# Mixing the first output tile inside the unit stage, opening the conv units' slots without a barrier, and a new order of the output stage

## The chip, the cores and the metric

The kernel runs on one core of one Trainium2 chip. The metric is the device time of one execution in microseconds (us). It computes in fp32 with matmuls on pairs of fp16 parts.

## What is computed

Two layers of a decoder, for one prompt of 2048 tokens and eight samples of eight tokens each. A layer is, cut to what matters here:

```python
h = rmsnorm(x, g_pre)
(...) = split_cols(h @ w_in)          # columns of four head groups
# A: short gated conv, B: gated linear attention, C: window attention, D: memory attention
mix = jnp.concatenate([a_out, b_out, c_out, d_out], axis=-1) @ w_out
y = x + rmsnorm(mix, g_post)
```

`y` of layer 0 is `x` of layer 1. The width is 1024.

## The kernel before

The tokens go through in four passes, of 1024 prompt tokens each: layer 0 first half, layer 0 second half, layer 1 first half, layer 1 second half. The second-half passes (2 and 4) also carry the 64 sample tokens. A pass has two stages, `units` (L1456) and `out` (L3018). Each of the five engines (TensorE or PE, ScalarE or ACT, VectorE or DVE, GpSimd or POOL, and SyncE or SP, which only issues transfers) goes through its own list in order and waits on semaphores.

**The unit stage.** `plan_units` (L461) writes one list of items with a forecast of each engine's time (`Forecast`, L171), and every engine walks the same list. Projections (`proj`, L2021) are cut in pieces between the attention work. The work of the head groups is divided into 16 slots; `begin` and `end` items open and close them. A `begin` that isn't `joined` makes PE, ACT, DVE and POOL wait until all four have ended the slot before (`all_steps_done`, L1642). Slots 8 and 9 and the last two, 14 and 15, belong to the conv units A; nearly all of the work of these is done by then, so that they hold no work in passes 1 and 3, and in passes 2 and 4 slot 15 holds two small transposes. At the end the planner places `o_split` (the last parts of `w_out`, split into a high and a low fp16 part by ACT and DVE, L2427 and L2676), `o_load` (in passes 2 and 4: kept parts of `w_out`, L1961, issued once slot 13 has ended on all engines), `o_x` (the next pass's first two rows of `x` and the norm weights `pre_g`, L1970 and L1971) and `o_mix`: the mix of the first output tile is split into `m_hi` (ACT, L2431) and `m_lo` (DVE, L2680). `o_mix` comes after slot 14. PE posts `left` after its last slot, once the PSUM banks 2 to 7 have been read (L2042).

**The output stage.** Its order is one hand-written list, `order` (L3056), of which each engine takes its share in that order. An output tile `t` is 128 tokens; there are 8, and 9 in passes 2 and 4, where tile 6 is the 64 sample tokens. The entries are:

- `("o", t, n)`: half `n` of the tile's product with `w_out` (PE L3147, 24 matmuls of 512 columns; sample tile L3136, 16), and ACT's sum of squares (L3214). For the sample tile ACT first copies the lower rows (L3208) and DVE adds them (L3274).
- `("mix", t)`: the split of mix tile `t` (ACT L3192, DVE L3259).
- `("fin", t)`: DVE's closing of a tile (L3280 to L3293, POOL's root L3119 between them), after which the tile's two banks are free for tile `t + 2` (L3295).
- `("xn", u)`: the next pass's norm of row tile `u`: ACT squares (L3180), DVE L3243 and L3244, POOL L3119, DVE L3248.
- `("h", u)`: the turn of that row tile (PE L3163, 8 transposes), ACT `h_hi` (L3223), DVE `h_lo` (L3303), and ACT's load of row tile `u + 2`.
- `("split", i)`: in passes 1 and 3, a part of `w_out` that the unit stage left over (one part, number 6; ACT L3196, DVE L3263). PE's second halves `("o", t, 1)` need the high and the low part of it (L3145).

There are no `xn` and `h` entries in pass 4, and in pass 2 there are eight of each (0 to 7). Passes 1 and 3 turn nine row tiles, of which the last is the samples. SP waits for all `left`, clears the unit stage's semaphores, and loads `post_g` and the first residual rows (L3077, L3079).

Of the kernel before, what the change touches and what calls it, by code (L numbers as in the profile page):

```python
# [33 lines left out]
ALU = mybir.AluOpType  # L34
# [426 lines left out]
def plan_units(with_sample):  # L461
# [137 lines left out]
    n_kept = [0]  # L599
    last_on_pe = [None]  # L600
# [215 lines left out]
    def follow():  # L816

        emit_parts()
        while raws and raws[0][0] <= fc.t["PE"]:
            wscale()  # L820
        while landing and max(landing[0][0], fc.at.get(("scaled", landing[0][1]), landing[0][0] if landing[0][1] < RING else float("inf"))) <= fc.t["PE"]:
            wsplit()
        while lows and lows[0][0] <= max(fc.t["PE"], fc.t["POOL"]):
            wlow()
        while out_landing and out_landing[0][0] <= fc.t["PE"] and (out_landing[0][1] >= RING or begun >= len(slots) - (2 if with_sample else 4)):
            emit(item("o_split", part=out_landing.pop(0)[1]))
        while waiting and rows_ready(waiting[0]) and rows_rest(waiting[0]):
            evict_next()
        while ahead and (max(ahead[0][0], fc.needs(ahead[0][1])) <= fc.t["PE"] + EARLY or not (left[ahead[0][1]["group"]] or running)):
            it = ahead.pop(0)[1]  # L830
            emit(it)
            turning[it["group"]] -= 1
# [35 lines left out]
    while ended < len(slots):  # L868
        follow()
        now = fc.t["PE"]  # L870
        if ended <= begun and not left[slots[ended]["index"]] and not any(x["step"]["slot"] == ended for x in main + side if "step" in x):
            emit(item("end", slot=ended, steps=[slots[ended]["main"]] + slots[ended]["side"]))
            ended += 1
            running = ended <= begun
            if not with_sample and ended == len(slots) - 4:
                out_loads += [2, 3]
                out_load("o_load", 0, after=ended)
                out_load("o_load", 1, after=ended)
            if with_sample and ended == len(slots) - 4:
                for part in (2, 3):  # L880
                    emit(item("o_load", part=part, after=ended))
            if with_sample and ended == len(slots) - 2:
                for part in (0, 1):
                    emit(item("o_load", part=part, after=ended))
            if ended == len(slots) - 2:
                emit(item("o_x"))
            if ended == len(slots) - 1:
                emit(item("o_mix"))
            continue
        if not running and not main:  # L890
            x = slots[begun + 1]
            if not (unread[x["index"]] or turning[x["index"]] or (heads and heads[0]["step"]["slot"] == x["index"])):
                main.append(item("begin", slot=x["index"], steps=[x["main"]] + x["side"], joined=False))
# [87 lines left out]
def hymba_step(nc, x_prompt, x_sample, state_conv, state_gla, cache_swa_k, cache_swa_v, cache_mem_k, cache_mem_v,  # L981
# [474 lines left out]
    def units(no, l, second, build, stored_so_far):  # L1456
# [527 lines left out]
        def on_tensor(pe):  # L1984
# [4 lines left out]
            for it in items:  # L1989
# [51 lines left out]
                elif kind == "end":  # L2041
                    if it["slot"] == n_slots - 1:  # L2042

                        for b in range(2, 8):
                            pe.wait_ge(bank_free[b], plan["uses"][b])
                        pe.drain().then_inc(left["pe"], 1)
                    else:
                        pe.drain().then_inc(step_pe, 1)
# [314 lines left out]
        def on_scalar(act):  # L2363
# [5 lines left out]
            for it in items:  # L2369
# [45 lines left out]
                elif kind == "end":  # L2415
                    if any(x["unit"] == "B" for x in it["steps"][1:]):

                        act.wait_ge(stored, 16 * stores)
                    act.drain().then_inc(left["act"] if it["slot"] == n_slots - 1 else step_act, 1)
# [8 lines left out]
                elif kind == "o_mix":  # L2428

                    all_steps_done(act, n_slots - 1)  # L2430
# [587 lines left out]
    def out(no, l, second, build, plan, n_stores):  # L3018
# [37 lines left out]
        order = [("xn", 0), ("mix", 1), ("o", 0, 0), ("h", 0), ("xn", 1)] + [("split", i) for i in late]  # L3056
        order += [("o", 1, 0), ("h", 1), ("xn", 2), ("o", 0, 1), ("fin", 0), ("mix", 2), ("o", 1, 1), ("h", 2), ("xn", 3), ("fin", 1), ("mix", 3)]
        for t in range(2, tiles - 2):
            order += [("o", t, 0), ("xn", t + 2), ("o", t, 1), ("h", t + 1), ("fin", t), ("mix", t + 2)]
        u, v = tiles - 2, tiles - 1  # L3060
        order += [("o", u, 1), ("h", u + 1), ("xn", u + 2), ("o", v, 1), ("h", u + 2), ("next",), ("o", u, 0), ("fin", u)]
# [61 lines left out]
        def on_tensor(pe):  # L3123
            for x in order:
                if x[0] == "o":
                    _, t, n = x
                    b = out_bank(t, n)
                    if t >= 2:
                        pe.wait_ge(out_free[b], t // 2)
# [19 lines left out]
                    m.then_inc(out_full[b], 1)  # L3149
                elif x[0] == "h":  # L3150
# [19 lines left out]
        def on_scalar(act):  # L3170
# [3 lines left out]
            for x in order:  # L3174
# [7 lines left out]
                elif x[0] == "mix":  # L3182
# [3 lines left out]
                    if t == 1:  # L3186

                        for e in ("pe", "dve"):
                            act.wait_ge(left[e], no)
                    if t >= 2:  # L3190
                        act.wait_ge(out_full[out_bank(t, 1)], t // 2)
# [38 lines left out]
        def on_vector(dve):  # L3230
# [3 lines left out]
            if build is not None:  # L3234
                dve.wait_ge(pre_in, 16)
                link(ts(pre_g, pre_g, H_UP, None, ALU.mult))
            for x in order:
                if x[0] == "xn":
                    u = x[1]
                    r = size(u)  # L3240
                    z = st_h[0:r, u % 2]
# [7 lines left out]
                elif x[0] == "mix":  # L3249
# [5 lines left out]
                    if t >= 2:  # L3255

                        dve.wait_ge(out_full[out_bank(t, 1)], t // 2)
# [176 lines left out]
```

## Time and profile before

| what | value |
|---|---|
| three runs | 2083.31, 2091.59, 2093.31 us; median 2091.59 us |
| the profiled execution's own time | 2083.04 us |
| its span, first to last instruction | 2081.2 us |
| mean granted TensorE clock | 0.981 |

The span leaves 1.8 us around it. The profiled execution lies 8.6 us under the median of the three. In the rows below, times are us from the span's start; a row of the timeline has the start, the duration, the engine, the line, the operation, the operands and the count of what is merged in it, and in brackets the engine's idle time before it and what ended it. A merged row's duration ends with the modelled end of its last matmul, so the next row may begin somewhat earlier.

### The profile page before, as it was taken

The page shows a single profiled execution, that of the slowest core. Times are in us where ns is not written, and L with a number is a line of the kernel's source. Part 1 is how long each engine was busy: PE and PEld are TensorE (multiplying, and loading weights), DVE is VectorE, ACT ScalarE, POOL GpSimd, SP SyncE. Part 2 cuts the span into 40 slices and gives each one's busy share as a digit, 9 for nine tenths or more (in the row PEclk, how much of TensorE's full clock was granted, in tenths as well). Part 3 has the DMA queues.
Part 4 walks back from the last instruction along what each step waited for, and adds up shares of the span by engine and source line. Part 5 has one row for each costly group of instructions (what it writes and reads, how often), then busy time and mean ns, then how long its engine had stood idle before and what let it go on. Part 6 is the DMA issues. An engine that isn't in the chain of part 4 may idle for free. (4 is left out here: it accounts for less than half of the span.)

```text
span 2081.2 us, 42790 instructions
## 1 busy us (share of the span) xinstructions
PE 1964.5 (94%) x16314; PEld 1114.3 (54%) x16314; DVE 1278.5 (61%) x2845; ACT 881.4 (42%) x2175; POOL 331.4 (16%) x251
## 2 busy tenths in 40 slices
PE   9999899989999999998999997998999999999998
PEld 5455444445566666665544554444445676566643
DVE  5577675666357775555646776566644677747533
ACT  4555343544355333344436443354435453424322
POOL 1443324000000000000114343320100000000000
PEclk9999999999999999999999999999999999999999
DMA  7731245555621133365356232546554112434632
GB/s 264 185 102 44 81 102 142 132 169 190 165 62 33 47 85 97 86 144 162 137 146 157 72 87 67 138 106 156 197 185 107 62 33 64 98 83 108 144 113 91
DMA packets 327494, 241.66 MB, mean 116 GB/s; under 512 B 188630, under 2 KB 273116, under 8 KB 327260
## 3 DMA queue, kind: packets, MB, share of 16 engines
q1 hardware_dynamic: 324180, 228.34, 40.4%
q10 hardware_dynamic: 3112, 10.59, 1.6%
q8 instruction: 131, 2.15, 0.4%
q14 instruction: 71, 0.58, 0.1%
HBM read 136.60 MB, written 57.71 MB: 93 GB/s over the span
## 5 line engine op out<-in xcount | busy, mean ns | idle before, releaser
L2021 PE MATMUL bank<-h_hi,w_parts 128*128 128x512 f16 (+4 forms) x4240 | 835.1, 344 | 30.9 <-ACTq L2409 15.5
L2021 PEld LDWEIGHTS bank<-h_hi,w_parts 128*128 128x128 f16 (+1 forms) x4240 | 400.5, 98 | 383.3 <-issue 75.5
L2021 PE MATMUL bank<-h_lo,w_parts 128*128 128x512 f16 (+3 forms) x2160 | 436.1, 344 | 0.9
L2021 PEld LDWEIGHTS bank<-h_lo,w_parts 128*128 128x128 f16 (+1 forms) x2160 | 207.0, 98 | 176.4 <-issue 9.7
L3147 PE MATMUL bank<-scr_h,tb_h 128*128 128x512 f16 x768 | 177.6, 391 | 14.5 <-ACT tb_h L2431 9.5
L3147 PE MATMUL bank<-w_parts,tb_h 128*128 128x512 f16 x768 | 170.4, 380 | 1.6 <-DVEq L3295 1.6
L2408 ACT ACTIVATE tb<-bank 128x512 f32<-128x512 f32 (+1 forms) x140 | 71.9, 514 | 190.3 <-PE bank L2021 186.7
L2977 POOL TENSOR_SCALAR w_raw<-w_raw 128x1024 f32<-128x1024 f32 x46 | 131.9, 2875 | 74.9 <-DMA w_raw<-in_w_in 74.3
L3147 PEld LDWEIGHTS bank<-scr_h,tb_h 128*128 128x128 f16 x768 | 76.4, 100 | 107.3 <-issue 12.4
L2972 POOL TENSOR_TENSOR w_parts<-w_raw,w_parts 128x1024 f16<-128x1024 f32 x46 | 100.9, 2196 | 205.2 <-ACT w_parts L2381 204.4
L3214 ACT ACTIVATE junk<-bank 128x512 bf16<-128x512 f32 (+1 forms) x68 | 40.6, 597 | 219.3 <-PE bank L3147 206.7
L2543 ACT ACTIVATE bank<-bank,stat 128x256 f32<-128x256 f32 x256 | 113.7, 447 | 44.0 <-DVE stat L2906 43.6
L3147 PEld LDWEIGHTS bank<-w_parts,tb_h 128*128 128x128 f16 x768 | 74.9, 98 | 91.0 <-DVEq L3295 2.6
L2757 DVE COPY_PREDICATED scr<-level_mask,bank 128x128 f32<-128x128 uint8 (+1 forms) x332 | 116.6, 351 | 11.3
L2404 ACT ACTIVATE tb<-bank 128x512 f32<-128x512 f32 (+1 forms) x80 | 40.9, 511 | 154.5 <-PE bank L2021 121.8
L2994 POOL TENSOR_TENSOR stat_g<-stat_g,minus_half 128x8 f32<-128x8 f32 (+1 forms) x20 | 29.2, 1462 | 457.0 <-DVE stat_g L2805 457.0
L2655 DVE SCALAR_TENSOR_TENSOR tb<-tb,gate_raw 128x512 f32<-128x512 f32 (+1 forms) x80 | 54.4, 680 | 48.6 <-ACT gate_raw L2405 45.5
L2931 DVE SCALAR_TENSOR_TENSOR scr_h<-bank,stat,scr_h 128x256 f16<-128x256 f32 x160 | 66.2, 475 | 15.7 <-ACT scr_h L2554 14.4
L2554 ACT ACTIVATE scr_h<-bank,stat 128x256 f16<-128x256 f32 x160 | 62.8, 490 | 12.1 <-DVE stat L2918 11.1
L2753 DVE COPY_PREDICATED scr<-diag_mask,bank 128x256 f32<-128x256 uint8 (+1 forms) x68 | 29.6, 436 | 53.4 <-ACTq L2489 43.4
L2946 DVE SCALAR_TENSOR_TENSOR mix_t<-bank,tb 128x256 f32<-128x256 f32 x64 | 27.0, 423 | 55.1 <-PE bank L2321 31.7
L2494 ACT ACTIVATE scr<-bank 128x128 f32<-128x128 f32 (+1 forms) x68 | 18.5, 272 | 98.5 <-PE bank L2162 86.9
(338 smaller groups left out, 2723.6 us busy)
## 6 DMA issues: line engine op xcount, KB each, us to landing
w_in_kept<-w_parts SPq DMA_DIRECT2D x104, 256.0 KB, 3.2
w_parts<-w_in_kept SPq DMA_DIRECT2D x104, 256.0 KB, 2.9
w_raw<-in_w_in SPq DMA_DIRECT2D x48, 512.0 KB, 4.2
out<-scr SPq DMA_DIRECT2D x32, 512.0 KB, 2.6
scr<-in_x_prompt SPq DMA_DIRECT2D x16, 512.0 KB, 4.1
scr<-out SPq DMA_DIRECT2D x16, 512.0 KB, 4.4
rot<-out ACTq DMA_DIRECT2D x12, 512.0 KB, 4.0
mix_t<-in_x_prompt SPq DMA_DIRECT2D x8, 512.0 KB, 11.9
```

What stands on the lines that cost most here:

```text
L2021: m = mm(bank[b][0:m_w, 0:c1 - c0], w[:, k, 0:m_w], h[:, k, c0:c1], start=it["piece"] == 0 and k == 0, stop=it["piece"] == 2 and k == KT - 1)
L2404: fn(part_of(s, "z", pt), src, ACT.Tanh, scale=0.5 * UNSCALE).then_inc(tanh_done, 1)
L2408: fn(part_of(s, role, pt), src, ACT.Copy, scale=scale).then_inc(tile_copied, 1)
L2543: m = fn(at, at, ACT.Exp, bias=z[:, 4 + x:5 + x], scale=1.0 if unit == "C" else HD ** -0.5, accum_out=z[:, 12 + x:13 + x])
L2554: m = fn(hi[:, 256 * x:256 * x + 256], scores_of(it["of"], x), ACT.Copy, scale=z[:, 20 + x:21 + x])
L2655: link(stt(z, z, 1.0, raw_gate(span, pt), ALU.add, ALU.mult))
L2757: m = nc.vector.copy_predicated(a.rearrange("p h (m i r) -> p h m i r", i=2, r=v)[:, :, :, 1, :], mask.to_broadcast([w, 2, w // (2 * v), v ...
L2931: m = stt(lo[:, part], scores_of(it["of"], x), z[:, 20 + x:21 + x], hi[:, part], ALU.mult, ALU.subtract)
L2972: tt(lo_of(t), w_raw[:, t % RING, :, 0:split_width(t)], hi_of(t), ALU.subtract).then_inc(w_lo_done, 1)
L2977: nc.gpsimd.tensor_scalar(raw, raw, W_UP, None, ALU.mult).then_inc(w_scaled, 1)
L3147: m = nc.tensor.matmul(bank[b].rearrange("p (j n) -> p j n", j=RING), lhs[:, t % 2, k, :], rhs[:, :, k, :], start=j == 0 and k == 0, stop= ...
L3214: link(fn(junk[0:r], bank[out_bank(t, n)][0:r], ACT.Square, accum_out=st_o[0:r, t % 2, n:n + 1]))
```

## The change

`o_mix` is placed as soon as slot 12 has ended and the gate of conv unit A1's first half is in the list, and ACT then waits only for the slots up to 12 and for that gate. The `begin` of a slot that holds only units A is joined, and so waits for nobody. PE no longer waits for the banks at the end of its last slot: it takes banks 2 and 3 ahead of the first half tile of the output stage, banks 4 to 7 after it, and posts `left` there; ACT posts its own `left` after PE's last slot. The order of the output stage is rewritten: the first turn comes after three half tiles, `xn` stands one tile ahead of its turn instead of two (the one ahead of the last loop's end comes after the loop), and `mix` comes ahead of `fin`. The planner's list of pass 1 and 3 is otherwise made by the same rules, with the changed forecast.

```diff
@@ plan_units
+    mixed = [False]
@@ follow()
+        if not mixed[0] and ended >= len(slots) - 3 and ("evict", slots[-2]["main"]["n"], "z") in placed:
+            emit(item("o_mix"))
+            mixed[0] = True
@@ the planner's loop
             if ended == len(slots) - 2:
                 emit(item("o_x"))
-            if ended == len(slots) - 1:
-                emit(item("o_mix"))
             continue
...
             if not (unread[x["index"]] or turning[x["index"]] or (heads and heads[0]["step"]["slot"] == x["index"])):
-                main.append(item("begin", slot=x["index"], steps=[x["main"]] + x["side"], joined=False))
+                free = x["main"]["unit"] == "A" and all(s["unit"] == "A" for s in x["side"])
+                main.append(item("begin", slot=x["index"], steps=[x["main"]] + x["side"], joined=free))
@@ units, on_tensor, kind "end"
-                    if it["slot"] == n_slots - 1:
-
-                        for b in range(2, 8):
-                            pe.wait_ge(bank_free[b], plan["uses"][b])
-                        pe.drain().then_inc(left["pe"], 1)
-                    else:
-                        pe.drain().then_inc(step_pe, 1)
+                    pe.drain().then_inc(step_pe, 1)
@@ units, on_scalar, kinds "end" and "o_mix"
+                    if it["slot"] == n_slots - 1:
+
+                        act.wait_ge(step_pe, n_slots)
                     act.drain().then_inc(left["act"] if it["slot"] == n_slots - 1 else step_act, 1)
...
-                    all_steps_done(act, n_slots - 1)
+                    all_steps_done(act, n_slots - 3)
+                    gate_written(act, next(x["n"] for x in plan["steps"] if (x["unit"], x["g"], x["st"]) == ("A", 1, 0)))
                     fn(m_hi[:, 0], mix_t[:, :, 0:P], ACT.Copy, scale=M_UP).then_inc(mh_done, 1)
@@ out
-        order = [("xn", 0), ("mix", 1), ("o", 0, 0), ("h", 0), ("xn", 1)] + [("split", i) for i in late]
-        order += [("o", 1, 0), ("h", 1), ("xn", 2), ("o", 0, 1), ("fin", 0), ("mix", 2), ("o", 1, 1), ("h", 2), ("xn", 3), ("fin", 1), ("mix", 3)]
-        for t in range(2, tiles - 2):
-            order += [("o", t, 0), ("xn", t + 2), ("o", t, 1), ("h", t + 1), ("fin", t), ("mix", t + 2)]
+        first_o = ("o", 0, 0)
+        order = [("mix", 1), ("xn", 0), ("o", 0, 0), ("xn", 1)] + [("split", i) for i in late]
+        order += [("o", 1, 0), ("o", 0, 1), ("h", 0), ("mix", 2), ("fin", 0), ("o", 1, 1), ("h", 1), ("xn", 2), ("mix", 3), ("fin", 1)]
+        order += [("o", 2, 0), ("h", 2), ("xn", 3), ("o", 2, 1), ("h", 3), ("mix", 4), ("fin", 2)]
+        for t in range(3, tiles - 2):
+            order += [("o", t, 0), ("xn", t + 1), ("o", t, 1), ("h", t + 1), ("mix", t + 2), ("fin", t)]
         u, v = tiles - 2, tiles - 1
-        order += [("o", u, 1), ("h", u + 1), ("xn", u + 2), ("o", v, 1), ("h", u + 2), ("next",), ("o", u, 0), ("fin", u)]
+        order += [("xn", u + 1), ("o", u, 1), ("h", u + 1), ("xn", u + 2), ("o", v, 1), ("h", u + 2), ("next",), ("o", u, 0), ("fin", u)]
@@ out, on_tensor
+                    if x == first_o:
+                        for b in range(2, 4):
+                            pe.wait_ge(bank_free[b], plan["uses"][b])
...
+                    if x == first_o:
+
+                        for b in range(4, 8):
+                            pe.wait_ge(bank_free[b], plan["uses"][b])
+                        pe.drain().then_inc(left["pe"], 1)
@@ out, on_scalar, "mix" (on_vector likewise waits for both halves at t >= 2)
-                        for e in ("pe", "dve"):
-                            act.wait_ge(left[e], no)
+                        act.wait_ge(left["dve"], no)
                     if t >= 2:
-                        act.wait_ge(out_full[out_bank(t, 1)], t // 2)
+                        for n in range(2):
+                            act.wait_ge(out_full[out_bank(t, n)], t // 2)
@@ out, on_vector
-            if build is not None:
-                dve.wait_ge(pre_in, 16)
-                link(ts(pre_g, pre_g, H_UP, None, ALU.mult))
...
+                    if u == 0:
+                        dve.wait_ge(pre_in, 16)
+                        link(ts(pre_g, pre_g, H_UP, None, ALU.mult))
```

## Rows read from the trace of the kernel before

**Rows 1.** The page: busy time of the engines

```profile
PE 1964.5 (94%) x16314; PEld 1114.3 (54%) x16314; DVE 1278.5 (61%) x2845; ACT 881.4 (42%) x2175; POOL 331.4 (16%) x251
```

**Rows 2.** PE's waits, whole span: us in total, times, longest us

```profile
PE bank L3147 <- ACT tb_h L2431: 9.5, 2, 4.8
...
PE bank L3147 <- DMA scr_h<-w_out_kept: 5.0, 2, 2.6
...
PE bank L2021 <- PEq L2048: 3.8, 4, 1.3
...
PE bank L3163 <- DVE rot L3248: 3.7, 3, 1.8
```

**Rows 3.** Timeline of PE in pass 1's output stage

```profile
435.61 7.04 PE L3147 MATMUL bank<-scr_h,tb_h 128*128 128x512 f16 x24 [4.76 <-ACT tb_h L2431]
444.01 1.09 PE L3163 MATMUL bank<-ident,rot 128*128 128x128 f32 x8 [1.35 <-DVE rot L3248]
...
473.45 5.34 PE L3147 MATMUL bank<-scr_h,tb_h 128*128 128x512 f16 x24
...
483.81 1.04 PE L3163 MATMUL bank<-ident,rot 128*128 128x128 f32 x8
```

**Rows 4.** Timeline of PE in pass 2's output stage

```profile
966.16 8.09 PE L3147 MATMUL bank<-scr_h,tb_h 128*128 128x512 f16 x24 [2.42 <-DMA scr_h<-w_out_kept]
...
1037.03 1.04 PE L3163 MATMUL bank<-ident,rot 128*128 128x128 f32 x8
1037.91 3.62 PE L3136 MATMUL bank<-scr_h,tb_h 128*128 128x512 f16 x16
...
1044.81 1.04 PE L3163 MATMUL bank<-ident,rot 128*128 128x128 f32 x8
...
1052.65 5.35 PE L3147 MATMUL bank<-w_parts,tb_h 128*128 128x512 f16 x24 [1.62 <-DVEq L3295]
```

**Rows 5.** Timeline of DVE in pass 1's output stage

```profile
440.90 0.69 DVE L3236 TENSOR_SCALAR spare<-spare 128x1024 f32<-128x1024 f32 x1 [4.08 <-DMA spare<-in_norm_pre]
...
442.67 1.28 DVE L3248 SCALAR_TENSOR_TENSOR rot<-rot,st_h,spare 128x1024 f32<-128x1024 f32 x1 [0.69 <-POOL st_h L3119]
...
449.50 1.22 DVE L3263 SCALAR_TENSOR_TENSOR w_parts<-w_raw,w_parts 128x1024 f16<-128x1024 f32 x1
...
481.11 0.16 DVE L3243 TENSOR_TENSOR st_h<-st_h 128x1 f32<-128x1 f32 x1 [1.36 <-ACTq L3181]
...
482.12 1.29 DVE L3248 SCALAR_TENSOR_TENSOR rot<-rot,st_h,spare 128x1024 f32<-128x1024 f32 x1 [0.66 <-POOL st_h L3119]
485.37 1.29 DVE L3303 TENSOR_TENSOR h_lo<-bank,h_hi 128x512 f16<-128x512 f32 x2 [1.96 <-ACT h_hi L3223]
486.57 0.15 DVE L3280 TENSOR_TENSOR st_o<-st_o 128x1 f32<-128x1 f32 x1
...
488.08 1.28 DVE L3293 SCALAR_TENSOR_TENSOR scr<-bank,st_o,scr 128x1024 f32<-128x1024 f32 x1
489.76 1.23 DVE L3259 SCALAR_TENSOR_TENSOR tb_h<-mix_t,tb_h 128x1024 f16<-128x1024 f32 x1 [0.39 <-DVE scr L3293]
```

**Rows 6.** Timeline of ACT in the same stretch

```profile
485.93 1.06 ACT L3192 ACTIVATE tb_h<-mix_t 128x1024 f16<-128x1024 f32 x1
```

**Rows 7.** Timeline of DVE in pass 2, at the sample tile and the banks' release

```profile
1044.12 0.68 DVE L3274 TENSOR_TENSOR bank<-bank,tb 64x512 f32<-64x512 f32 x1
...
1051.17 1.28 DVE L3293 SCALAR_TENSOR_TENSOR scr<-bank,st_o,scr 64x1024 f32<-64x1024 f32 x1
```

**Rows 8.** Timeline of SP in pass 2, at the end of its unit stage

```profile
961.53 0.81 SPq L1961 DMA_DIRECT2D scr_h<-w_out_kept  x2
```

**Rows 9.** Timeline of PE in pass 4, the last halves

```profile
2053.20 10.70 PE L3147 MATMUL bank<-w_parts,tb_h 128*128 128x512 f16 x48
```

**Rows 10.** Timeline of DVE in pass 2, where `o_mix` will come

```profile
944.42 0.42 DVE L2620 SCALAR_TENSOR_TENSOR tb<-bank,tb 128x256 f32<-128x256 f32 x1 [0.42 <-issue]
```

**Rows 11.** Windows: busy of PE, PEld, DVE, ACT, POOL, then the granted clock (PEclk)

```profile
436.00:438.00 2.00, 2.00 (x7) 0.64 (x5) 0.81 (x1) 0.45 (x1) 0.00 (x0) 0.50 0.99 387
```

More of the change, by code:

```diff
@@ L3123, in on_tensor @@
         def on_tensor(pe):
-            for x in order:
+            for i, x in enumerate(order):
                 if x[0] == "o":
@@ L3127, in on_tensor @@
                     b = out_bank(t, n)
+                    if x == first_o:
+                        for b in range(2, 4):
+                            pe.wait_ge(bank_free[b], plan["uses"][b])
+                        b = out_bank(t, n)
                     if t >= 2:
@@ L3255, in on_vector @@
                     if t >= 2:
-                        dve.wait_ge(out_full[out_bank(t, 1)], t // 2)
+                        for n in range(2):
+                            dve.wait_ge(out_full[out_bank(t, n)], t // 2)
                     m_low = m_lo[:, t % 2] if r == P else m_hi[:, t % 2, :, r:2 * r]
```

## The prediction

> **What bounds the kernel.** I read the page first: PE is busy for 94% of the span, and no other engine for more than 61% [rows 1]. So a change pays or costs only by what it does to PE's pauses. PE's waits come next [rows 2]: the ones this diff touches are the two before the first output half of passes 1 and 3 (9.5 us), the two for the kept `w_out` in passes 2 and 4 (5.0 us), the three for the first turn (3.7 us) and the four behind its own slot ends (3.8 us). The timeline shows how dense the rest is: two halves take 10.36 us [rows 3], so 5.18 each; a turn takes 0.88, a sample half 3.45 [rows 4]. After pass 1's first turn PE doesn't pause until the stage's end. The output stage has no slack on PE to swallow a late norm or a late release.
>
> **The distances that decide.** All are read from one steady tile [rows 3, 5, 6], counted from a turn's start S = 483.81. DVE's low part comes at S+1.6; ACT's `mix` runs from S+2.1 to S+3.2; `fin` begins on DVE at S+2.8, its last operation at S+4.3, and DVE is free at S+5.95, so `fin` holds it 3.2. The banks are free 1.48 after that last operation starts [rows 4, 7]. With `mix` first, DVE waits for ACT until S+3.2, works 1.23 to S+4.4, and `fin` follows: banks free at S+7.4, DVE free at S+7.6. A norm: from the end of a half at 478.63 to DVE's first step 2.48 (ACT's sums, of which about 0.9 is the half's and 1.5 the row's), then 2.3 on DVE and POOL until 483.41; in all 4.8 against the 5.2 of the half that covers it. The steady loop thus holds with 0.4 to spare, and costs nothing.
>
> **Passes 1 and 3, start.** The idle 4.76 and, since `o_mix` is done, the first wait both go; PE starts at about 431.3 in place of 435.61. But the second half of tile 0 now comes third, and needs the left-over part's low split. That sits on DVE behind `xn` 0 and `xn` 1. `xn` 0 ends at 443.95, since `pre_g` only lands at 440.90 [rows 5]; its load waits for slot 13 as before. Then `xn` 1 (2.3) and the split (1.22): 447.4. PE waits there in two pieces (0.7, 3.0), does the remaining 16 of 24 matmuls (3.45) and turns row 0 at 450.9. To the first half of tile 3 it has four turns and three halves: 19.1. Two new waits: tile 2's first half comes 6.9 after that turn and the banks at 7.4, so 0.5; and the turn of row 3 waits for DVE, which goes `xn` 2 (free at 5.7 after turn 1, an estimate from the same distances), `mix` 3 (6.9), `fin` 1 (10.1), low part and `xn` 3 (13.6) where PE is there at 12.6: 1.1. So tile 3 starts at 471.5, and not at 473.45 [rows 3]: -1.9 in each pass, **-3.8**.
>
> **Passes 1 and 3, slots 8 and 9.** PE's four waits of 3.8 us behind its slot ends [rows 2] shrink to the drains, about 0.25 each: **-2.8**. Ends: 0 (another wait takes over) and -3.8.
>
> **Passes 1 and 3, end.** The steady loop leaves `xn` 7 behind `fin` 5. After the turn of row 6, DVE is free at S+7.6 and ends the norm at S+9.9; PE has one half and wants the turn at S+6.1. Before, the norm was a tile ahead. +3.9 each, **+7.8**.
>
> **Passes 2 and 4, start.** Tile 0 waits for kept `w_out` parts that SP issues after slot 13 [rows 8] and that land for 966.16 [rows 4]. Early mixing moves neither. The transposes of slot 15 only move inside the idle time. Pass 2 has the drain for `left` (0.25), the same two waits (1.6), and loses its wait at the first turn (3.7 less 1.35 and about 1.8: 0.5): **+1.35**. Pass 4 has the drain, and, without turns, banks at 6.3 (square 0.9, `mix` 1.06 and 1.23, `fin` 3.0) where PE comes at 5.2: **+1.35**.
>
> **Pass 2, sample tile.** `xn` 7 now stands between the two sample halves, which last 6.9 together and have an exchange of their own: DVE free at S+7.6, sample add 0.68 [rows 7], ACT 0.8 and 1.5, norm 2.3: S+12.9, where PE is there at S+7.8 (before: no pause at 1044.81 [rows 4]). The second sample half's add, the turn's copies, `mix` 8 and `fin` 6 follow, so tile 8 starts at about S+20.9 in place of S+15.6: **+5.3**. Pass 4 has no norms, but `mix` 7 ahead of `fin` 5 and `mix` 8 ahead of `fin` 6 bring the banks 3.1 after PE wants them, where before it waited 0.2 or 0.3 (10.70 for two halves [rows 9]): **+3.1**.
>
> **`o_mix` inside slot 13.** DVE meets it after slot 12 and must wait for ACT (1.06), then work 1.23. In pass 2 that stands ahead of the operation at 944.42, which frees a projection bank and had 0.42 of idle time [rows 10]: 2 us late, on PE 0 to 1.5. I take 0.7 in each of passes 2 and 4: **+1.4**. In passes 1 and 3 DVE idles before the end and I take 0; ends 0 and 1 each.
>
> **The clock.** After 4.76 of idle time PE's 24 matmuls took 7.04 for 5.34, at a granted clock of 0.50, the level of 1.2 GHz [rows 3, 11]: 1.7 lost. After 1.62 nothing was lost (5.35), after 2.42 that followed other idle time 2.75 [rows 4]. The new pauses of 3.9, 3.9 and 5.2 are nearest the first: 1.7 each, **+5.1**. The new ones of 3.0 to 3.1 (three) lie between; I take 0, ends 0 and 1.7 each.
>
> The Trainium skill, TensorE: Matmul & The Clock Gate, section "HAM oscillation — how this bites in real kernels", warns that a loop whose PE waits again and again restarts cold each time. By it all six would pay, 10.2 in place of 5.1; of the trace's pauses the long ones agree and that of 1.62 doesn't.
>
> **Sum.** -3.8 - 2.8 + 7.8 + 1.35 + 1.35 + 5.3 + 3.1 + 1.4 + 5.1 = +18.8, on the profiled execution's 2083.04: 2101.8. That execution is 8.55 under the median of the runs shown; on the median it is **2110.4 us**.
>
> **The rivals.**
>
> *The start's gain without the new waits.* If the low split of the left-over part were ready for the third half (that asks for `pre_g` some 3.5 us earlier, or for that part not to be left over) and the late norms were covered, passes 1 and 3 would start tile 3 at about 466.2, 7.3 earlier each: with the slots -17.4, 2074.2. Against it: DVE works in the order of the list, and the distances are measured ones. It decides at the point where `xn` 0 ends before 440. Chance 0.1.
>
> *No clock price, half the waits.* The planner's list changes from slot 8 on, and its shifts can be of either sign; with no cold restart and nothing lost in slot 13, +12.3 is left, and with the sample tile's waits halved 8: 2099.6, within what a measurement can tell, which for this kernel is about 0.5% or 10.5 us. Chance 0.3.
>
> *The forecast costs more.* All short pauses pay the clock as well (5.1), the slot gain is eaten (2.8) and slot 13 costs 1.5 and 1 (3.6): +30, 2121.9. Chance 0.15.
>
> *The change doesn't do what it says* only in passes 2 and 4, where the start stays with the loads; that is in the sum.
>
> **How the numbers follow.** The forecast has 0.45, and with the third rival 0.6 for slower by over 0.5%; the second is the 0.3 for no difference, the first the 0.1 for faster. The range leaves out the first rival and the far end of the third: from 2090 (the unfavourable terms halved and both gains whole) to 2125.
>
> **What would show it.** PE's timeline in pass 1: the output stage starts near 431, pauses of 0.7 and 3 inside tile 0's second half, the turn of row 0 near 451. Waits of PE L3163 on DVE L3248: about 1.1, 3.9 in passes 1 and 3, about 5 in pass 2. Waits of PE L3147 on DVE's drain L3295: 0.5 in three passes, 1.1 and 3.1 in pass 4. It would be wrong if the turn of row 7 doesn't wait in any pass, if PE waits for bank releases less than before, or if the unit stages shift by more than 3 us each.

## The result, and the profile after

The changed kernel takes 2114.45 us (median of four runs, 2110.59 to 2116.55). The kernel before takes 2090.95 us in four runs on the same chip. The ratio is 1.0117, with a 95% interval of 1.0099 to 1.0136: 23.5 us slower. The profiled execution took 2116.55 us (span 2114.8, mean granted clock 0.973), that of before 2083.04 (0.981). So the two profiles lie 33.6 us apart, 10 more than the medians. The clock accounts for it: one minus the granted clock, times the span, is 39.5 us in the profile of before and 57.1 us in that of after; over all runs whose clock is on record it is 47.9 us (46 runs of before) and 53.3 us (four of after).

The page's busy line, as [rows 1]:

```profile
PE 1982.3 (94%) x16314; PEld 1123.2 (53%) x16314; DVE 1277.7 (60%) x2845; ACT 880.2 (42%) x2175; POOL 331.7 (16%) x251
```

The work is the same, instruction for instruction in number. The busy time of PE grew by 17.8 us, about what the clock lost between the two profiles (17.6). The rest, 15.8 us, is idle time of PE. The windows show where: each pass's unit stage (from its first projection to its last value matmul), then its output stage. The columns are the window, its length, and busy time with the count for PE, PEld, DVE, ACT and POOL, then the granted clock, the DMA share and GB/s. Before:

```profile
49.70:430.00 380.30, 358.26 (x3008) 183.33 (x3008) 256.00 (x554) 173.80 (x399) 125.53 (x58) 0.99 0.45 114
430.00:529.91 99.91, 93.54 (x469) 46.07 (x469) 58.53 (x87) 44.06 (x97) 8.80 (x16) 0.98 0.57 189
529.91:958.70 428.79, 410.36 (x4120) 269.35 (x4122) 260.81 (x691) 175.53 (x496) 19.64 (x28) 0.98 0.37 88
958.70:1068.73 110.03, 101.87 (x518) 49.53 (x515) 60.35 (x92) 44.27 (x101) 8.78 (x16) 0.95 0.46 152
...
1550.72:1975.21 424.49, 409.78 (x4120) 268.89 (x4122) 260.70 (x691) 175.56 (x496) 19.64 (x28) 0.98 0.35 87
1975.21:2081.20 105.99, 93.17 (x454) 41.94 (x450) 38.52 (x53) 23.48 (x52) 4.95 (x9) 0.95 0.29 105
```

After:

```profile
49.81:433.52 383.71, 361.70 (x3008) 186.25 (x3008) 257.87 (x556) 175.96 (x402) 125.98 (x58) 0.98 0.43 112
433.52:537.16 103.64, 95.94 (x469) 46.34 (x470) 57.10 (x86) 41.47 (x94) 8.80 (x16) 0.97 0.58 194
537.16:970.67 433.51, 413.18 (x4121) 270.62 (x4122) 261.81 (x692) 176.64 (x497) 19.62 (x28) 0.98 0.35 85
970.67:1086.71 116.04, 103.41 (x519) 50.35 (x515) 58.96 (x91) 42.76 (x100) 8.79 (x16) 0.94 0.43 144
...
1574.38:2003.88 429.50, 411.91 (x4120) 269.70 (x4122) 261.74 (x692) 176.60 (x497) 19.64 (x28) 0.98 0.35 86
2003.88:2114.76 110.88, 94.28 (x454) 42.02 (x450) 36.76 (x52) 22.43 (x51) 4.95 (x9) 0.95 0.29 100
```

Pass 3, left out, is like pass 1: unit stage 381.61 before and 384.50 after, output stage 100.38 and 103.17. The output stages lost 3.7, 6.0, 2.8 and 4.9 us: 17.4 in all. The unit stages lost 3.4, 4.7, 2.9 and 5.0: 16.0 in all, although their own wait had been taken away. But of these 16.0 us 10.9 are busy time of PE, which is the clock's share; the idle time in the unit stages (length less busy time of PE) grew by only 5.1 us, from 77.7 to 82.8. In the output stages it grew by 10.0, from 34.2 to 44.2. PE's waits, as [rows 2]:

```profile
PE bank L3175 <- DVE rot L3260: 14.9, 6, 4.6
PE bank L3154 <- DMA scr_h<-w_out_kept: 10.2, 2, 5.1
...
PE bank L3154 <- DVE w_parts L3276: 4.2, 2, 2.3
...
PE bank L2024 <- DVEq L2625: 3.7, 4, 1.7
PE bank L3154 <- DVEq L3308: 3.6, 2, 2.8
PE bank L2326 <- DMA rot_h<-rot_h: 3.5, 2, 2.2
```

The waits for the first mix (9.5) and behind PE's own slot ends (3.8) are gone. In their place stand: turns that wait for norms, 14.9 us (was 3.7); the second half that waits for the low split of the left-over part, 4.2; banks released late in pass 4, 3.6; and two in the unit stage that had no such row before, 3.7 and 3.5. The kept loads show 10.2 for 5.0, but the stage gets no longer by it: PE starts 7.62 us after the last value matmul in pass 2 (978.29 less 970.67) and took 7.46 before (966.16 less 958.70 [rows 4]). The transposes of slot 15 no longer cut this idle time in two.

PE's timeline at the start of pass 1's output stage, then the turns of rows 3 and 7; the last two rows are the turn of row 7 in pass 2 and a release in pass 4:

```profile
433.52 0.85 PE L2326 MATMUL bank<-rot_h,mem_v 128*64 128x256 f16 x12 [1.27 <-DMA rot_h<-rot_h]
...
434.99 12.49 PE L3154 MATMUL bank<-scr_h,tb_h 128*128 128x512 f16 x48 [0.62 <-issue]
447.31 1.89 PE L3154 MATMUL bank<-w_parts,tb_h 128*128 128x512 f16 x8
451.53 5.30 PE L3154 MATMUL bank<-w_parts,tb_h 128*128 128x512 f16 x16 [2.33 <-DVE w_parts L3276]
456.67 1.04 PE L3175 MATMUL bank<-ident,rot 128*128 128x128 f32 x8
...
476.17 1.09 PE L3175 MATMUL bank<-ident,rot 128*128 128x128 f32 x8 [1.01 <-DVE rot L3260]
477.10 5.34 PE L3154 MATMUL bank<-scr_h,tb_h 128*128 128x512 f16 x24
...
519.52 1.09 PE L3175 MATMUL bank<-ident,rot 128*128 128x128 f32 x8 [3.38 <-DVE rot L3260]
...
1062.11 1.97 PE L3175 MATMUL bank<-ident,rot 128*128 128x128 f32 x8 [4.63 <-DVE rot L3260]
...
2092.09 5.35 PE L3154 MATMUL bank<-w_parts,tb_h 128*128 128x512 f16 x24 [2.78 <-DVEq L3308]
```

DVE in pass 1, at the new place of `o_mix`, at the start of the output stage, and at row 7:

```profile
420.57 1.23 DVE L2681 SCALAR_TENSOR_TENSOR tb_h<-mix_t,tb_h 128x1024 f16<-128x1024 f32 x1 [4.17 <-ACT tb_h L2432]
...
428.56 1.65 DVE L2932 SCALAR_TENSOR_TENSOR rot_h<-bank,stat,rot_h 128x256 f16<-128x256 f32 x4
...
444.98 0.69 DVE L3252 TENSOR_SCALAR spare<-spare 128x1024 f32<-128x1024 f32 x1 [4.08 <-DMA spare<-in_norm_pre]
446.75 1.28 DVE L3260 SCALAR_TENSOR_TENSOR rot<-rot,st_h,spare 128x1024 f32<-128x1024 f32 x1 [0.69 <-POOL st_h L3122]
450.17 1.22 DVE L3276 SCALAR_TENSOR_TENSOR w_parts<-w_raw,w_parts 128x1024 f16<-128x1024 f32 x1
...
512.91 1.23 DVE L3272 SCALAR_TENSOR_TENSOR tb_h<-mix_t,tb_h 128x1024 f16<-128x1024 f32 x1
...
515.57 1.28 DVE L3306 SCALAR_TENSOR_TENSOR scr<-bank,st_o,scr 128x1024 f32<-128x1024 f32 x1
...
518.18 1.28 DVE L3260 SCALAR_TENSOR_TENSOR rot<-rot,st_h,spare 128x1024 f32<-128x1024 f32 x1 [0.66 <-POOL st_h L3122]
```

The last three rows are one queue: `mix`, the closing of a tile, and only then the norm that PE waits for from 516.1 on. The first two show what the prediction overlooked. DVE stands 4.17 us at the low half of `o_mix` until ACT's high half is written, and the work behind it on DVE comes late. The operation at 428.56 ran at 422.74 before:

```profile
422.74 1.66 DVE L2931 SCALAR_TENSOR_TENSOR rot_h<-bank,stat,rot_h 128x256 f16<-128x256 f32 x4
```

Its result goes through a transfer to PE's last value matmuls, and PE waits 1.27 us for it, where it had no such wait. That these matmuls come at 433.52 in place of 430.00 is mostly the clock. A row of 24 matmuls just ahead of slot 8 (L2318, before L2321), far ahead of `o_mix`, already comes at 317.46 in place of 314.26: from 240 to 250 us the granted clock is 0.50 in this profile and 0.76 in that of before, and from 270 to 280 us 0.83 and 1.00.

### The profile page after: what moved, and what is told of

It reads as the page before. It is cut to its first block, busy times and chain, and to the rows that moved or that the text cites. A ratio compares the mean times of both kernels' runs of the same rounds, so it can differ in the third digit from the quotient of the medians.

```text
span 2114.8 us, 42723 instructions
## 1 busy us (share of the span) xinstructions
PE 1982.3 (94%) x16314; PEld 1123.2 (53%) x16314; DVE 1277.7 (60%) x2845; ACT 880.2 (42%) x2175; POOL 331.7 (16%) x251
## 4 chain that ended last, share of the span: by engine, by line
PE 66%; DVE 16%; ACT 5%; issue 4%; DMA 3%; SPq 2%; ACTq 1%; POOL 1%; DVEq 1%; POOLq 0%
PE bank L2024 38%; PE bank L3154 12%; PE bank L2107 2%; ACT bank L2544 2%; PE bank L1371 1%; PE bank L2273 1%; PE bank L2318 1%; PE bank L2267 1%; PE bank L2066 1%; ACTq L2406 1%; PE bank L3175 1%; PE bank L2159 1%; DVE scr_h L2932 1%; PE bank L2093 1%; DVE tb L2656 1%
## 5 line engine op out<-in xcount | busy, mean ns | idle before, releaser
L3154 PE MATMUL bank<-scr_h,tb_h 128*128 128x512 f16 x768 | 177.7, 390 | 12.7 <-DMA scr_h<-w_out_kept 10.2
L3154 PE MATMUL bank<-w_parts,tb_h 128*128 128x512 f16 x768 | 175.2, 386 | 7.0 <-DVE w_parts L3276 4.2
L2544 ACT ACTIVATE bank<-bank,stat 128x256 f32<-128x256 f32 x256 | 113.7, 447 | 45.0 <-DVE stat L2907 44.2
L3154 PEld LDWEIGHTS bank<-w_parts,tb_h 128*128 128x128 f16 x768 | 76.1, 99 | 99.1 <-issue 10.7
L3272 DVE SCALAR_TENSOR_TENSOR tb_h<-mix_t,tb_h 128x1024 f16<-128x1024 f32 (+1 forms) x30 | 35.7, 1188 | 61.1 <-ACT tb_h L3204 59.1
L2555 ACT ACTIVATE scr_h<-bank,stat 128x256 f16<-128x256 f32 x160 | 62.8, 490 | 12.3 <-DVE stat L2919 11.2
L3316 DVE TENSOR_TENSOR h_lo<-bank,h_hi 128x512 f16<-128x512 f32 (+1 forms) x52 | 32.6, 666 | 54.4 <-ACT h_hi L3235 52.9
L3122 POOL TENSOR_TENSOR st_o<-st_o,minus_half 128x1 f32<-128x1 f32 (+1 forms) x34 | 18.7, 549 | 295.5 <-DVE st_o L3294 295.5
```

The costliest lines, as they stand in the source:

```text
L2544: m = fn(at, at, ACT.Exp, bias=z[:, 4 + x:5 + x], scale=1.0 if unit == "C" else HD ** -0.5, accum_out=z[:, 12 + x:13 + x])
L2555: m = fn(hi[:, 256 * x:256 * x + 256], scores_of(it["of"], x), ACT.Copy, scale=z[:, 20 + x:21 + x])
L3154: m = nc.tensor.matmul(bank[b].rearrange("p (j n) -> p j n", j=RING), lhs[:, t % 2, k, :], rhs[:, :, k, :], start=j == 0 and k == 0, stop= ...
```

## The experiments

All ratios are to the kernel before, timed on the same chip as the run. The runs are called e1 to e12; e11 stands ahead of e5, beside the one it belongs to. The median of the kernel before was 2088.39 us beside e1 to e4, 2089.26 beside e5 to e8 and 2086.37 beside e9 to e12. "Units" and "output" are the sums over the four stages of the experiment's own profile. One profile carries its own clock, so these sums are good to some 8 us at best: e2 has the unit stages of before unchanged, and they take 1623.6 us in its profile, where that of before has 1615.2. Where it matters, PE's idle time in the same stages is given too, since it leaves out the busy time that a low clock adds.

**The two parts of the change alone.** First the change without its new order (e1):

```diff
-        order = [("mix", 1), ("xn", 0), ("o", 0, 0), ("xn", 1)] + [("split", i) for i in late]
+        order = [("xn", 0), ("mix", 1), ("o", 0, 0), ("h", 0), ("xn", 1)] + [("split", i) for i in late]
...
```

> The changed kernel with the output stage's order of before; o_mix inside slot 13, the joined begins and the moved bank waits stay. In the two profiles the output stages (from the last value matmul of slot 13 on) hold +17.5 us of the difference and the unit stages +16.0, while the medians differ by 23.5. Theory 1 (the new order costs, by the late norms and late bank releases): about 2100 us, 14 under the changed kernel, and PE never waits for a row's norm ahead of a turn but for the first. Theory 2 (the unit stage's new list costs, the order is harmless): 2112 to 2115 us.

Measured: 2098.69 us, 1.0052 (1.0028 to 1.0076); units 1626.7, output 421.7. PE in pass 1's output stage, and DVE there:

```profile
430.43 5.34 PE L3153 MATMUL bank<-scr_h,tb_h 128*128 128x512 f16 x24 [0.59 <-issue]
...
443.87 1.97 PE L3174 MATMUL bank<-ident,rot 128*128 128x128 f32 x8 [8.10 <-DVE rot L3259]
```

```profile
440.76 0.69 DVE L3251 TENSOR_SCALAR spare<-spare 128x1024 f32<-128x1024 f32 x1 [7.22 <-DMA spare<-in_norm_pre]
```

PE starts 5.2 us earlier (430.43 for 435.61) and turns row 0 only 0.14 us earlier (443.87 for 444.01 [rows 3]): `pre_g` lands at 440.76, where it landed at 440.90 [rows 5]. The idle 4.76 turned into a longer wait for the norm. The parts without the new order thus earn nothing and cost 0.3 to 0.8%; an order with more work ahead of the first turn was needed for that gain, and the new order is what costs most. The reverse, the new order in the kernel before (e2):

```diff
-        order = [("xn", 0), ("mix", 1), ("o", 0, 0), ("h", 0), ("xn", 1)] + [("split", i) for i in late]
+        order = [("mix", 1), ("xn", 0), ("o", 0, 0), ("xn", 1)] + [("split", i) for i in late]
...
```

> The kernel before with the new order of the output stage and nothing else. Theory 1: the waits of PE ahead of turns (1.0, 3.4, 4.6 us) and for bank releases in pass 4 (0.8 and 2.8) come with it, and the start gains nothing since o_mix still ends the idle time: 2105 to 2110 us. Theory 2: within 3 us of 2091.

Measured: 2108.90 us, 1.0101 (1.0073 to 1.0129); units 1623.6, output 434.8, after's 433.8. The order by itself makes nearly the whole loss. The two excesses, 0.0052 and 0.0101, add up to more than the changed kernel's 0.0117, but not by more than their intervals allow.

**The barrier of slots 8, 9, 14 and 15 back (e3).**

```diff
-                main.append(item("begin", slot=x["index"], steps=[x["main"]] + x["side"], joined=free))
+                main.append(item("begin", slot=x["index"], steps=[x["main"]] + x["side"], joined=False))
```

> The changed kernel with every begin of a conv unit's slot waiting for all engines again. Theory 1 (the joined begins save PE's two waits behind slots 7 and 8 in passes 1 and 3, 3.8 us less the drains): 2116 to 2118 us. Theory 2 (what they change in the planner's forecast moves items for the worse): 2108 to 2112 us.

Measured: 2115.38 us, 1.0139 (1.0107 to 1.0171). The interval overlaps that of the changed kernel (1.0099 to 1.0136), so the run doesn't decide. It also did more than I meant. The barriers of the last slots, which hold no work, are back too, and behind one of them PE waited at the start of the output stage in passes 1 and 3, for 6.9 and 6.2 us:

```profile
PE bank L3153 <- PEq L2044: 13.1, 2, 6.9
```

A run that brings the barrier back for slots 8 and 9 alone comes below.

**The mix late again (e4)**, everything else as changed:

```diff
-        if not mixed[0] and ended >= len(slots) - 3 and ("evict", slots[-2]["main"]["n"], "z") in placed:
-            emit(item("o_mix"))
-            mixed[0] = True
...
+            if ended == len(slots) - 1:
+                emit(item("o_mix"))
...
-                    all_steps_done(act, n_slots - 3)
+                    all_steps_done(act, n_slots - 1)
```

> The changed kernel with o_mix back behind slot 14 and its wait for all slots up to 14. DVE's wait of 4.2 us for ACT's half of it in slot 13 goes. Theory 1 (that wait is what makes the unit stages longer): 2103 to 2108 us, and PE's idle time ahead of the first output half of passes 1 and 3 is back without making the first turn later, since that hangs on the low split behind xn 0 and xn 1. Theory 2 (the early mix is worth its place): 2118 us or more.

Measured: 2111.79 us, 1.0116 (1.0086 to 1.0145). Units 1618.6, which is 12.6 less than after; output 440.2, which is 6.4 more. The unit stages get their time back, as my theory said. But the time as a whole hardly moves, and my range was missed. PE's idle time in the unit stages falls by 9.1 us (82.8 to 73.7) and rises by 3.6 in the output stages; the clock takes the rest back. One minus the granted clock, times the span, is 61.2 us in the mean of these four runs and 53.3 in those of the changed kernel. The idle time at the start of the stage is back, in passes 1 and 3:

```profile
433.79 13.18 PE L3153 MATMUL bank<-scr_h,tb_h 128*128 128x512 f16 x48 [4.76 <-ACT tb_h L2431]
...
451.99 1.04 PE L3174 MATMUL bank<-ident,rot 128*128 128x128 f32 x8
```

48 matmuls take 13.18 us after it, where e9, without a pause, takes 10.80 for as many.

**The low half of the mix later (e11).** The two halves of `o_mix` become two items, and DVE's comes after the last use of its results that PE waits for:

```diff
+        if low_due[0] and ("value", next(x["n"] for x in steps if (x["unit"], x["g"], x["st"]) == ("D", 1, 1)), 0) in placed:
+            emit(item("o_mix_lo"))
+            low_due[0] = False
...
-                elif kind == "o_mix":
+                elif kind == "o_mix_lo":
```

> The changed kernel with DVE's half of o_mix as an item of its own, placed behind the value product of the last D step's first half instead of right behind ACT's half. Theory 1 (DVE stands 4.2 us for ACT in slot 13 and so delays bank releases and the last probabilities' transposes): the unit stages are about 10 us shorter in all, PE's waits for the transposed probabilities (1.3 and 2.2 us) go, the medians 5 to 10 us under the changed kernel: ratio to before 1.007 to 1.009. Rival (it is ACT's half or the changed forecast that costs, or the clock takes it back, as it did in e4): 1.0115.

Measured: 2105.74 us, 1.0085 (1.0069 to 1.0101); units 1619.4, output 436.2. DVE in pass 1:

```profile
431.42 1.21 DVE L2689 SCALAR_TENSOR_TENSOR tb_h<-mix_t,tb_h 128x1024 f16<-128x1024 f32 x1
```

The wait of 4.17 us is gone. PE's idle time in the unit stages falls from 82.8 to 74.4 us, and the kernel lies 0.3% nearer to the one before, while its runs lose as much to the clock (54.0 us) as those of the changed kernel (53.3). That is what the low half's place costs. In pass 1, where both profiles have the same low clock between 240 and 280 us, the last value matmuls come 1.6 us earlier (431.91).

**The order mended, one piece at a time.** `fin` ahead of `mix`, as before the change (e5):

```diff
-[..., ("h", t + 1), ("mix", t + 2), ("fin", t)]
+[..., ("h", t + 1), ("fin", t), ("mix", t + 2)]
```

> The changed kernel with every tile's closing (fin) ahead of the next mix again, nothing else undone. Theory 1 (each queue's order makes the waits): PE's waits for bank releases in pass 4 (0.8 and 2.8 us) go, the turn of row 7 still waits 3 us and more, since its norm stays behind both; about 5 us under the changed kernel (ratio to before 1.009). Theory 3 (the clock and the unit stages make most of the difference, single waits move elsewhere): no change, 1.0117.

Measured: 2111.55 us, 1.0112 (1.0095 to 1.0129). Pass 4's output stage takes 106.9 in place of 110.9 (before 105.99), so the late releases were due to this swap. The waits of the turns stay (15.2), and the total is within the noise of the changed kernel's: less gained than I expected, and by the time alone the outcome of theory 3. Of the waits only the releases' 3.6 us are gone, and those for the low split are 5.6 in place of 4.2.

The norms two tiles ahead of their turn, as before the change (e6):

```diff
-            order += [("o", t, 0), ("xn", t + 1), ("o", t, 1), ("h", t + 1), ("mix", t + 2), ("fin", t)]
+            order += [("o", t, 0), ("xn", t + 2), ("o", t, 1), ("h", t + 1), ("mix", t + 2), ("fin", t)]
...
-        order += [("xn", u + 1), ("o", u, 1), ...]
+        order += [("o", u, 1), ...]
```

> The changed kernel with the norms two tiles ahead of their turn in the steady loop again (xn 4 behind turn 3, xn t+2 in the loop). Theory 1: the waits of 3.4, 4.6 and 3.4 us at the turn of row 7 go and with them some lost clock, 11 to 15 us under the changed kernel, ratio to before 1.005 to 1.006. Theory 3: 1.010 or more.

Measured: 2102.24 us, 1.0065 (1.0050 to 1.0081); output stages 98.0, 113.6, 98.1 and 110.3. PE's waits:

```profile
PE bank L3154 <- DVEq L3308: 6.6, 3, 3.0
...
PE bank L3175 <- DVE rot L3260: 3.5, 3, 1.5
```

The turns wait 3.5 us for 14.9. This is the largest single term. The releases rise from 3.6 to 6.6: in pass 2 as well, PE now arrives before `fin` behind `mix`.

Both pieces, and the left-over split ahead of the norms (e7):

```diff
-        order = [("mix", 1), ("xn", 0), ("o", 0, 0), ("xn", 1)] + [("split", i) for i in late]
+        order = [("mix", 1)] + [("split", i) for i in late] + [("xn", 0), ("o", 0, 0), ("xn", 1)]
...
```

> The changed kernel with fin ahead of mix, norms two ahead, and the left-over part's split ahead of xn 0 instead of behind xn 1. Theory 1: no wait of PE in the output stages beyond the first half tile and the kept parts' loads in passes 2 and 4; the waits for the split (2.3 and 1.9 us) are gone, tile 3 of pass 1 starts 4 us earlier than in the changed kernel after the same unit stage: 2088 to 2093 us, ratio 1.000 to 1.002, the rest of the difference being the unit stages. Theory 3: 1.006 or more.

Measured: 2086.67 us (10 runs), 0.9987 (0.9974 to 1.0001); output stages 94.3, 110.8, 94.2 and 106.7. That is faster than I expected (2088 to 2093). All three new waits of the output stage are gone or small, and the output stages of passes 1 and 3 are 5.6 and 6.2 us shorter than before the change. The same with the mix late (e8):

> As e7, with o_mix back behind slot 14. Theory 1: the unit stages lose DVE's wait for ACT (about 10 us in all four, from the profiles of e1 and e4 less their clock), PE's idle time of 4.8 us before the output stages of passes 1 and 3 comes back: 2081 to 2087 us, ratio 0.996 to 0.999, the only one under the kernel before. Rival (the idle time costs as much again through the clock): 2089 us and more.

Measured: 2090.86 us (10 runs), 1.0009 (0.9995 to 1.0023), where I had expected 2081 to 2087. Units 1615.1, as before the change; output 418.4, which is 12.3 more than with the mix early. This is e4's miss again, on a mended order. The mix early costs some 13 us of unit stages in one profile and saves 12 of output stages (8.8 and 8.0 us of PE's idle time), so neither place alone wins by its waits. The 4.2 us between the medians of e7 and e8 fit the clock: 50.8 us are lost to it in the mean of e8's runs, 44.6 in e7's. So the rival of this expectation is the one that the runs bear out.

**A version that takes both gains (e9).** The order of e7; the mix early, with its low half later, only in passes 1 and 3, where it ends a wait; behind slot 14 in passes 2 and 4, where the loads set the start:

```diff
-        if not mixed[0] and ended >= ...
+        if not with_sample and not mixed[0] and ended >= ...
...
+            if with_sample and ended == len(slots) - 1:
+                emit(item("o_mix"))
+                emit(item("o_mix_lo"))
```

> The output order of e7 (its output stages of passes 1 and 3 took 94.3 and 94.2 us where before has 99.9 and 100.4), o_mix inside slot 13 in passes 1 and 3 only and with DVE's half placed later, behind slot 14 in passes 2 and 4 (e8's unit stages took 1615.1 us together, e7's 1628.0). Theory 1: the two gains add: 2077 to 2083 us, ratio 0.994 to 0.997. Rival (as in e8, idle time that is gone in one place comes back through clock or loads): 0.999 to 1.001.

Measured: 2078.33 us (2076.09 to 2081.10), 0.9954 (0.9937 to 0.9970); units 1622.5, output 406.5. The output stages are as short as e7's (406.1); PE's idle time is 79.5 us in the unit stages and 27.3 in the output stages, where before has 77.7 and 34.2. It beats the kernel before by 0.3 to 0.6% and the changed one by more. PE and DVE in pass 1:

```profile
429.18 10.80 PE L3165 MATMUL bank<-scr_h,tb_h 128*128 128x512 f16 x48 [0.59 <-issue]
439.82 5.34 PE L3165 MATMUL bank<-w_parts,tb_h 128*128 128x512 f16 x24
445.00 1.04 PE L3186 MATMUL bank<-ident,rot 128*128 128x128 f32 x8
```

```profile
434.24 1.22 DVE L3287 SCALAR_TENSOR_TENSOR w_parts<-w_raw,w_parts 128x1024 f16<-128x1024 f32 x1
...
440.93 1.28 DVE L3271 SCALAR_TENSOR_TENSOR rot<-rot,st_h,spare 128x1024 f32<-128x1024 f32 x1 [0.70 <-POOL st_h L3133]
```

The three halves run without a pause from 429.18 to 445.00, the split is ready at 435.5 and row 0's norm at 442.2, both ahead of their use.

Two variations of it. The barrier back for slots 8 and 9 alone (e10):

```diff
-                free = x["main"]["unit"] == "A" and ...
+                free = x["index"] >= 14 and x["main"]["unit"] == "A" and ...
```

> As e9_best, with slots 8 and 9 waiting for all engines again. Theory 1: PE's four waits behind the ends of slots 7 and 8, 3.8 us, are back, less the drains: 2 to 3 us over e9_best. Rival (the list made by the changed forecast eats it): the same time or less.

Measured: 2079.96 us, 0.9958 (0.9943 to 0.9974). That the joined slots 8 and 9 save 2 to 3 us can't be seen. In the profiles PE's idle time in the unit stages is even 4.2 us less with the barrier (75.3 for 79.5). And the load of `pre_g` ahead of the two rows of `x` (e12):

> As e9_best, with the norm weights' load issued ahead of the two row tiles' loads. Since the first turn now comes three halves after the start, about 15.5 us, and the weights land 10 us after it, theory 1 says no change against e9_best within 1 us. Rival (the first turn still hangs on them): 1 us or more faster, and a wait of the first turn on the norm in e9_best.

Measured: 2078.18 us, 0.9959 (0.9944 to 0.9973): no change. With three halves ahead of the first turn, the landing of `pre_g` no longer sets anything.

## Why the prediction was right, and where it wasn't

The forecast was 2110.4 us, and the median is 2114.45; the direction, the range and the order as the main cause hold. The sum was +18.8; the medians are 23.5 apart. But the parts didn't all come out, and one of the three signs of being wrong did: the unit stages shift by more than 3 us in three passes of four (3.4, 4.7, 2.9 and 5.0). The clock makes 10.9 of these 16.0 us; the rest is idle time of PE, to which `o_mix` adds (below).

**The end of passes 1 and 3, and the sample tile**: right. The turn of row 7 waits 3.38 and 3.37 us (3.9 forecast) and in pass 2 4.63 (5.1), for the norm queued behind `mix` and `fin`, as worked out. The run with the norms two ahead takes 11.4 us of these waits away.

**Start of passes 1 and 3**: right in kind, though everything came later. The turn of row 3 waits 1.01 (1.1 forecast), tile 2's release 0.2 (0.5), the split 2.33 in pass 1 and 1.86 in pass 3 (two pieces of 0.7 and 3.0 in each). The turn of row 0 comes at 456.67 in place of 450.9: the unit stage ended 3.5 us later, and the 16 matmuls behind the split took 5.30 in pass 1, where an undisturbed row of 16 takes 3.62 [rows 4] (3.61 in pass 3). Counted from the last value matmul, the output stage of pass 1 is 3.7 us longer, and the forecast of its terms, -1.9 + 3.9 + 1.7, says the same. That the sums agree is luck. I had the first halves run at full clock once the idle 4.76 was gone, but the first 48 matmuls took 12.49 us in pass 1 and 12.48 in pass 3, where e7 and e9 take 10.80; and the 1.7 for the clock at row 7 didn't come in pass 1.

**Pass 4's releases**: 0.78 and 2.78 (1.1 and 3.1), caused by the swap of `fin` and `mix`, as e5 shows by removing them. **The starts of passes 2 and 4** stay with the loads, as forecast. Together the forecast's terms for the output stages make 20.2, clock included; the profiles show 17.4, and most of the difference lies in pass 2 (6.0 for 8.35).

**`o_mix` inside slot 13**: this is the step that failed. I took 0.7 us in passes 2 and 4, and nothing in passes 1 and 3 because DVE is idle there before the end. I had counted ACT's 1.06 as the whole wait. ACT itself reaches its half late, so that DVE stood 4.17 us in pass 1 (1.75 in pass 2). And DVE's idle time before the end isn't free: the operation behind it feeds a transfer that feeds PE. In the run with the low half later the median falls by 0.32% of about 2090, some 7 us, and PE's idle time in the unit stages of the profile by 8.4; the forecast had 1.4.

**Slots 8 and 9**: right at the place, not shown in the time. After, one short pause is left at the place in pass 1,

```profile
318.66 1.03 PE L2024 MATMUL bank<-h_hi,w_parts 128*128 128x512 f16 x4 [0.34 <-issue]
```

where the profile of before has two, of 0.73 and 1.28 us, at 318.73 and 321.05. So 1.7 us is saved at the place in that pass, for a forecast of 1.4. With the barrier back the time doesn't change by what a run can tell, and the idle times of the unit stages point both ways: 79.5 joined and 75.3 with the barrier (e9 and e10), but 73.7 and 74.3 joined (e4 and e8) where before and e2, with it, have 77.7 and 75.9. So the term of -2.8 isn't shown.

**The clock**: +5.1 forecast, +5.4 measured over all runs (53.3 less 47.9). That the size is right is in part luck: the clock was lost at other places than I had priced, see below. Without the clock the medians differ by 18.1 where the terms sum to 13.7, and the some 7 us of `o_mix` in place of 1.4 make up for the gap.

**The rivals.** The gain of the start without new waits didn't come, since the split waited until 450.17. But most of it was there to be had: e9 has three halves ahead of its first turn at 445.0, and from the last value matmuls to the first half of tile 3 it takes 37.8 us where before takes 43.5, so 5.7 less where that rival had 7.3. It came from the split placed ahead of the norms, and not from an earlier `pre_g`. The second rival, with no price for the clock and half the waits of the sample tile covered, is ruled out: the waits are 4.63 and 2.78 us, the turn of row 7 in pass 2 is followed by 2.3 us of lost clock, and the range of the runs (2110.59 to 2116.55) lies above its 2099.6. The costlier rival, +30, named slot 13 as one of its causes with 3.6; it was right about the place.

**What stays open.** Why the unit stages of e4 and of before, with the same place for `o_mix`, differ by 3.4 us in their profiles, and the effect of joining slots 8 and 9: both are below what these runs resolve. e8 has the order's waits mended and the unit stages of before, and still isn't faster than the kernel before; its profile accounts for that (output 418.4 against 416.3, with the idle 4.8 back in passes 1 and 3), and its runs' clock (50.8 us lost), but no run isolates it. Why the first 48 matmuls of an output stage lost 1.7 us of clock in the changed kernel and not in e7, with much the same pauses ahead of them, is open too.

## What to carry to other kernels

Where an idle time is removed at the head of a stage, look for the next thing that is late, and put the work in the order in which it becomes due: here the 4.76 us moved whole to the next wait (8.10) until the split was put ahead of the norm. An item that two engines do in turn (a high half, then what is left over) should be two items in a planner: placed as one, the second engine stands at it with everything queued behind. A norm or a release that was covered with 0.4 us to spare shows its margin only where the pattern ends, at the last row and at the odd tile, so cost those edges by themselves.

## What the hardware did that I had not expected

A pause of PE has no fixed price in clock. After 2.33 us of idle, 16 matmuls took 5.30 us in place of 3.62. After 3.38 us in pass 1 nothing was lost; after 3.37 us in pass 3 the turn took 1.86 in place of 1.04 and the next 24 matmuls 6.29 in place of 5.34:

```profile
1555.03 1.86 PE L3175 MATMUL bank<-ident,rot 128*128 128x128 f32 x8 [3.37 <-DVE rot L3260]
1556.69 6.29 PE L3154 MATMUL bank<-w_parts,tb_h 128*128 128x512 f16 x24
```

Nor does it take one long pause. In the changed kernel 48 matmuls took 12.49 us behind two pauses of 1.27 and 0.62 us. In e7, in pass 3, as many took 10.80 behind 2.07 and 0.59:

```profile
1452.53 0.85 PE L2326 MATMUL bank<-rot_h,mem_v 128*64 128x256 f16 x12 [2.07 <-DMA rot_h<-rot_h]
1453.97 10.80 PE L3154 MATMUL bank<-scr_h,tb_h 128*128 128x512 f16 x48 [0.59 <-issue]
```

The windows behind the pauses of 2.33, 3.38 and 4.63 us (the granted clock is the third number from the end; 0.50 is 1.2 GHz, 1.00 is 2.4 GHz):

```profile
450.00:455.00 5.00, 3.47 (x11) 1.37 (x12) 1.39 (x2) 0.00 (x0) 0.00 (x0) 0.77 0.04 13
519.00:523.00 4.00, 3.48 (x20) 2.09 (x21) 1.94 (x5) 2.41 (x6) 0.00 (x0) 1.00 0.63 152
1062.00:1066.00 4.00, 3.89 (x13) 2.46 (x14) 2.35 (x5) 2.82 (x5) 0.00 (x0) 0.50 0.01 4
```

The three pauses that I priced at 1.7 each cost about 0, 1.8 and, for pass 2 (turn 1.97 for 1.04, 48 matmuls 12.11 for 10.7), 2.3: 4.1 together for 5.1. The Trainium skill, TensorE: Matmul & The Clock Gate, section "HAM oscillation — how this bites in real kernels", has a loop that waits for a transfer at every step start each step cold. The three longest waits for a norm don't agree with a rule for each wait: 4.63 us was followed by the lower clock, and of the two of 3.38 and 3.37 us only that in pass 3. The waits of 1.01 and 1.49 us at row 3, which cost nothing, are shorter than the waits that the section describes, and so was the 1.62 that the prediction held against it.

The clock also differs from run to run of the same kernel. The nine runs of before beside the first four experiments have spans of 2077.5 us at a granted clock of 0.981 up to 2089.9 at 0.975. These 12 us are half of what the whole change did, and such a difference is why the two profiles alone would have overstated it by 10 us.
